# Projection stage of a transformer block in float32: its matmuls as three one-pass products of high and low parts, values made turned, keys and values kept in DRAM

## The reference, cut to what matters

```python
h = modulate(rms_norm(x, norm1_w), sh1, sc1)
hc = modulate(rms_norm(xc, norm1_w), csh1, csc1)
proj = h @ w_in                                   # q 512, k 128, v 128, hyena 1536 columns
kv_c = hc @ w_in[:, K_OFF:HY_OFF]                 # context keys and values
kc = rms_norm(split_heads(kv_c[..., :KV_W], N_KV_HEADS), k_norm_w)
q = rope_2d(rms_norm(split_heads(proj[..., :K_OFF], N_HEADS), q_norm_w), ang_r, ang_c)
k = rope_2d(rms_norm(split_heads(proj[..., K_OFF:V_OFF], N_KV_HEADS), k_norm_w), ang_r, ang_c)
v = split_heads(proj[..., V_OFF:HY_OFF], N_KV_HEADS)
att = windowed_attention(q, k, v, kc, vc, attn_sink)
hy = hyena_mixer(proj[..., HY_OFF:], ...)         # starts with a 3-tap convolution over the tokens
```

## Time and profile before

| | |
|---|---|
| median of 3 runs | 2721.09 us (2717.26 to 2721.49) |
| the profiled execution's own time | 2725.7 us |
| its span in the trace | 2723.9 us |
| mean granted clock of PE | 0.941 of full |
| busy: PE, PEld, DVE, ACT, POOL | 2376.9, 1452.7, 1333.2, 1097.9, 504.3 us |
| L800 (hyena products) | 768 matmuls, 336.0 us |
| L747 (key and query products) | 320 matmuls of 512 tokens, 142.7 us |
| L775 (values) | 288 matmuls, 28.9 and 3.7 us |

### The profile page before, as it was taken

How to read it: one execution, slowest core, us unless ns; L and a number is a source line. 1 busy time by engine, 2 the same in 40 slices (tenths; PEclk the granted TensorE clock), 3 DMA queues, 4 the chain that set the end, 5 groups by cost and what they waited for, 6 DMA issues and landing times. The chain is left out here.

```text
span 2723.9 us, 42063 instructions
## 1 busy us (share of the span) xinstructions
PE 2376.9 (87%) x14659; PEld 1452.7 (53%) x14660; DVE 1333.2 (49%) x2332; ACT 1097.9 (40%) x2039; POOL 504.3 (19%) x842
## 2 busy tenths in 40 slices
PE   4888999999996999858999999945988999889997
PEld 1333743444443666534666666643655666555664
DVE  4634376121121555434555555424655775555674
ACT  2543121111112444324554555414645665455563
POOL 1652011000000111000122222231222122222221
PEclk8988999999996999858999999967999999999999
DMA  4985121111117344241222222107988889786994
GB/s 162 333 258 144 30 78 43 39 54 47 31 47 184 87 111 110 51 150 54 58 64 60 66 69 71 51 31 284 319 271 285 290 301 324 237 262 210 313 317 125
DMA packets 239821, 410.02 MB, mean 151 GB/s; under 512 B 25220, under 2 KB 128140, under 8 KB 234884
## 3 DMA queue, kind: packets, MB, share of 16 engines
q1 hardware_dynamic: 161461, 334.11, 36.8%
q0 software_dynamic: 18608, 44.71, 6.9%
q10 hardware_dynamic: 59616, 29.38, 4.0%
HBM read 342.08 MB, written 74.49 MB: 153 GB/s over the span
## 5 line engine op out<-in xcount | busy, mean ns | idle before, releaser
L800 PE MATMUL ps_proj<-sb_hT,sb_win 128*128 128x512 f32 x768 | 336.0, 597 | 7.6 <-DVE sb_rot L906 6.0
L800 PEld LDWEIGHTS ps_proj<-sb_hT,sb_win 128*128 128x128 f32 x768 | 145.7, 192 | 189.8 <-issue 182.9
L2369 PE MATMUL ps_byp<-sb_w,sb_gT 128*128 128x512 f32 x512 | 232.8, 597 | 1.5 <-ACT sb_gT L2172 1.5
L2078 DVE TENSOR_TENSOR sb_w1l<-sb_raw,sb_w1h 128x1024 fp32r<-128x1024 f32 x128 | 148.2, 1220 | 172.8 <-ACT sb_w1h L2142 172.8
L1812 DVE CUSTOM_DVE_ANT_0 sb_pr<-ps_S,sb_mask 128x640 f32<-128x640 f32 x128 | 105.2, 822 | 128.5 <-PE ps_S L1636 128.5
L1634 PE MATMUL ps_S<-sb_kT,sb_qb 64*128 64x256 f32 x256 | 97.7, 465 | 67.1 <-DVE sb_mx L1812 49.6
L1731 ACT ACTIVATE sb_pr<-sb_pr,sb_nm 128x640 f32<-128x640 f32 x128 | 106.3, 830 | 117.8 <-DVE sb_nm L1816 117.8
L916 DVE TENSOR_SCALAR sb_hyv<-sb_hu,sb_cols 128x2048 f32<-128x2048 f32 x12 | 16.2, 1347 | 281.0 <-ACT sb_hu L869 281.0
L2078 DVE TENSOR_TENSOR sb_w3l<-sb_raw,sb_w3h 128x1024 fp32r<-128x1024 f32 x128 | 150.8, 1221 | 5.2 <-ACT sb_w3h L2142 5.2
L1346 POOL TENSOR_TENSOR sb_zr<-sb_zr,sb_skip 128x512 f32<-128x512 f32 x32 | 40.0, 1282 | 605.5 <-DMA sb_skip<-in_hy_skip 454.8
L747 PE MATMUL ps_proj<-sb_hT,sb_win 128*128 128x512 f32 x320 | 142.7, 600 | 8.9 <-DMA sb_win<-in_w_in 8.3
(11 more groups left out here) (292 smaller groups left out, 5007.7 us busy)
## 6 DMA issues: line engine op xcount, KB each, us to landing
sb_raw<-in_exp_w SPq DMA_DIRECT2D x64, 2048.0 KB, 17.0
sb_w<-in_exp_w SPq DMA_DIRECT2D x32, 2048.0 KB
sb_ada<-in_ada_w SPq DMA_DIRECT2D x16, 1536.0 KB, 7.8
scr_filt<-sb_fout ACTq DMA_DIRECT2D x128, 128.0 KB, 3.4
sb_yh<-scr_filt SPq DMA_DIRECT2D x64, 256.0 KB, 5.1
sb_win<-in_w_in SPq DMA_DIRECT2D x9, 1024.0 KB, 5.8
sb_xr<-in_x SPq DMA_DIRECT2D x16, 512.0 KB
sb_gt<-scr_hy_in SPq DMA_DIRECT2D x8, 1024.0 KB
```

What stands on the lines that cost most here:

```text
L800: ins = pe.matmul(mp[:, (NQ + n) % 4, :], w[:, pc % 3, k, (ct % 2) * P:(ct % 2 + 1) * P], g.hT[:, k, c * 512:(c + 1) * 512], start=(k == 0 ...
L2078: ve.tensor_tensor(piece(low[m], part), piece(raw13[par][:, m], part), piece(high[m], part).bitcast(F32), ALU.subtract).then_inc(lo[m], 1)
L2369: ins = pe.matmul(yp[:, part, :], gT[:, f, :], w2[par][:, f, part * 512:(part + 1) * 512], start=(f == 0), stop=(f == FT - 1), skip_group_ ...
```

## The change

All products of the stage are made of operands split in two parts: `high`, the value rounded to the one-pass type `float32r`, and `low`, the rest, also in that type. A product is then, for each of the 8 slices, `wh*high + wh*low + wl*high`: 24 instructions of one pass. What else changes:

- Splitting. ACT writes the high parts of the weights (`weights_high`) and of the rows (`rows_high`), DVE the low parts of the weights (`weights_low`) and of slices 0 to 4 of the rows, POOL those of slices 5 to 7 (`rows_low`). The low parts overwrite the originals. Modulation is now DVE's for slices 0 to 4 and POOL's for 5 to 7. The context comes first, then the chunks, and the later chunks are modulated and split between the rotations of the first key blocks (L942, L949 and L1020, L1027).
- The jobs are one list, which PE, ACT and DVE follow: context keys and values, then key and value chunks in alternation, then queries, then hyena. Values are made like all others and turned by PE (`turn_values`, L814).
- The root is taken by ACT from the mean square itself, straight from PSUM, with `eps` as its bias (`norm_root`), and the reciprocal comes after it on DVE; L895 is gone. In ACT's list `norm_root(m - 1)` stands behind `weigh(m)`, as before.
- Two weight pieces in place of three, one buffer for the convolution's input and one for its output in place of two, one for the turned result. `hcTh`, rope tables and the next stage's table `fwd` use the same memory one after the other, so the table is loaded only after the last rotation, and two more weight pieces wait behind it in SP's list.
- Keys and values go to DRAM, and `stage4` loads them back (four more transfers on SP, L1166) into memory that the rows had.

The core of the diff:

```diff
@@ stage3, order of the jobs
-    qk = [("k", 4, n) for n in range(CH)] + [("kc", 4, 0)] + [("q", ct, n) for ct in range(4) for n in range(CH)]
-    hy = [(ct, n) for ct in range(12) for n in range(CH)]
+    jobs = [("kc", 4, 0), ("vc", 5, 0), ("k", 4, 0), ("tc", 5, 0), ("v", 5, 0)]
+    for n in range(1, CH):
+        jobs += [("k", 4, n), ("t", 5, n - 1), ("v", 5, n)]
+    jobs += [("q", 0, 0), ("t", 5, CH - 1)] + [("q", ct, n) for ct in range(4) for n in range(CH)][1:]
+    jobs += [("h", 6 + ct, n) for ct in range(12) for n in range(CH)]
...
@@ PE, a product
-                for k in range(KT):
-                    rhs = g.hcT[:, k, :] if kind == "kc" else g.hT[:, k, c * 512:(c + 1) * 512]
-                    ins = pe.matmul(mp[:, n % 4, 0:N], w[:, pc % 3, k, (ct % 2) * P:(ct % 2 + 1) * P], rhs,
-                                    start=(k == 0), stop=(k == KT - 1))
+                if r == first_job[pc]:
+                    pe.wait_ge(w_lo, pc + 1)
+                if kind in ("kc", "k"):
+                    pe.wait_ge(lo_v, part + 1)
+                    pe.wait_ge(lo_p, part + 1)
...
+                for k in range(KT):
+                    a, b = wh[:, pc % 2, k, cs], wl[:, pc % 2, k, cs]
+                    pe.matmul(mp[:, r % 4, 0:N], a, high[:, k, :], start=(k == 0), stop=False)
+                    pe.matmul(mp[:, r % 4, 0:N], a, low[:, k, :], start=False, stop=False)
+                    ins = pe.matmul(mp[:, r % 4, 0:N], b, high[:, k, :], start=False, stop=(k == KT - 1))
...
@@ ACT
+            def weights_high(n):
+                act.wait_ge(ldw[n % 2], 16 * (n // 2 + 1))
+                act.copy(wh[:, n % 2, :, :], w[:, n % 2, :, :]).then_inc(w_hi, 1)
+            def rows_high(n):
+                x, high, _, _ = rows(n)
+                act.wait_ge(mod_v, n + 1)
+                act.copy(high[:, 0:5, :], x[:, 0:5, :]).then_inc(h_hi, 1)
+                act.wait_ge(mod_p, n + 1)
+                act.copy(high[:, 5:KT, :], x[:, 5:KT, :]).then_inc(h_hi, 1)
...
+            for job in jobs:
...
+                if kind in ("kc", "k", "q"):
+                    m = qk.index(job)
+                    weigh(m)
+                    if m >= 1:
+                        norm_root(m - 1)
...
+                if kind in ("vc", "v") and split <= CH:
+                    rows_high(split)
+                    split += 1
...
@@ DVE
+            modulate(0)
+            modulate(1)
+            rows_low(0)
+            weights_low(0)
+            modulate(2)
+            rows_low(1)
+            for n in range(NQ):
+                rotate(n)
+                if n + 3 <= CH:
+                    modulate(n + 3)
+                if n + 2 <= CH:
+                    rows_low(n + 2)
...
@@ POOL
+                    pool.dma_start(dst, src).then_inc(st_q[n % 2], 16)
+                if n + 3 <= CH:
+                    modulate(n + 3)
+                if n + 2 <= CH:
+                    rows_low(n + 2)
...
@@ stage4, SP, behind load_z(2)
+            for dst, src in ((g.kT[0:HD, :, P:P + T], g.k_dram), (g.kT[HD:2 * HD, :, 0:C], g.kc_dram),
+                             (g.v[:, 0:2, :], g.v_dram[:, NT:NT + 2, :]), (g.v[:, 3:3 + NT, :], g.v_dram[:, 0:NT, :])):
+                sp.dma_start(dst, src).then_inc(ld_kv, 16)
```

More of the change, by code:

```diff
@@ new lines, in stage3 @@
+    first_job = [min(at[job] for job in piece_of if piece_of[job] == n) for n in range(len(pieces))]
+    last_job = [max(at[job] for job in piece_of if piece_of[job] == n) for n in range(len(pieces))]
+    split_at = [None] + [min(first_job[n - 1] + 4, last_job[n - 1]) if n > 1 else at["k", 4, 2] for n in range(1, len(pieces))]
+    with e.stage() as st:
+        with nc.sbuf_tensor("sb_win", [P, 2, KT, PW], F32) as w:
+            pass
+        wl = e.sb(st, "winl", [P, 2, KT, PW], F32R)
+        wh = e.sb(st, "winh", [P, 2, KT, PW], F32R)
+        hh = e.sb(st, "hTh", [P, KT, T], F32R)
@@ new lines, in product @@
+            def product(job):
+                kind, ct, n = job
+                r, pc = at[job], piece_of[job]
+                part = n + 1 if kind in ("k", "v") else 0
+                cs = slice((ct % 2) * P, (ct % 2 + 1) * P)
+                if r == first_job[pc]:
[3 more added lines that the diff above has]
+                    pe.wait_ge(lo_p, part + 1)
+                bank(r)
+                if kind in ("kc", "vc"):
+                    high, low, N = hch, hcl, C
+                else:
+                    _, high, low, _ = rows(n + 1)
+                    N = 512
@@ new lines, in _ @@
+            normed = 0
+            for job in jobs:
+                kind, ct, n = job
+                if kind in ("tc", "t"):
+                    turn_values(job)
+                    continue
+                product(job)
+                if normed < NQ and at[qk[normed]] < at[job]:
+                    norm(normed)
+                    normed += 1
+                if kind == "h" and (ct, n) == (6, 0):
+                    pe.wait_ge(auxr, NQ)
+                    pe.wait_ge(root, NQ)
+                if kind == "h" and ct >= 7 and n == 1:
+                    turn(ct - 7)
@@ L872, in _ @@
             turned(11)
-            for b in range(2):
-                act.wait_ge(st_z[b], 16 * 6)
-            act.wait_ge(ld_f, 16)
+            act.wait_ge(st_z, 16 * 12)
         @block.vector
@@ L929, in _ @@
+            modulate(0)
+            modulate(1)
+            rows_low(0)
+            modulate(2)
+            rows_low(1)
             for n, (kind, ct, c) in enumerate(qk):
-                N = C if kind == "kc" else 512
+                N = width(kind)
                 pool.wait_ge(rotd, n + 1)
```

367 lines of the change are left out of this document (204 added, 163 removed).

## The result

| | before | after |
|---|---|---|
| median of the runs | 2719.18 us (4 runs, 2715.13 to 2721.49) | 2639.81 us (4 runs, 2628.94 to 2644.11) |
| ratio to before, 95% interval | | 0.9704 (0.9671 to 0.9736) |
| the profiled execution's own time, span | 2725.7, 2723.9 us | 2641.22, 2639.5 us |
| projection stage in its trace | 230.69 to 829.09: 598.4 us | 231.65 to 754.80: 523.1 us |
| first query product, from the stage's start | 81.1 us | 104.5 us |

The change is faster, by 79.4 us in the medians. The mechanism was the one forecast; sizes were off. The stage saves 75.2 us where 58.5 were forecast, and more than half of that difference lies in its start.

What follows compares the result with a forecast made beforehand. PE's matmul count and spacing were taken to bound the stage. Savings 20.6 + 5.2 + 65.2 less 32.5 made 58.5 us: 2725.7 to 2667.2, and 2662 as median, which lies 4.6 below the profiled execution; range 2640 to 2680.

Steps and rivals of the forecast that it cites:

- Costs 32.5: Stage start up to the first query product: 113.7 us after the change against 81.2 before, a loss of 32.5 us.
- the turns between DVE and POOL: Splitting a chunk at the start: DVE and POOL take turns at SBUF, holding both for 11.0 us a chunk.
- POOL's sending and products of the next rotation in between 1.5: Wait before key chunk 1: 1.5 us for this work, within 18.1 us from the end of key chunk 0.
- Key chunk 0: Key product at the stage's start: waits for 11.0 us of splitting from 14.3, starts 25.5, ends 31.1.
- Products behind gaps: Key products of chunks 1 to 3: PE's clock is low behind the gap, so 8.0 us for each product.
- 46 spacings, 0.2333 us each: Hyena and query products: expert stage's one-pass spacing carried over, 24 instructions in 5.60 us, saving 1.27 us a product.
- The queries: First query to first hyena product: 136.6 us before, 115.9 after, with DVE's work covered; saves 20.6 us.
- side by side: Rival, chance 0.28: DVE and POOL don't exclude each other or POOL modulates in 0.4; first query product at 99 to 101, 2648.
- Join: First to second hyena product: 14.8 us before, 9.6 after, as only the three rope products are waited for; saves 5.2 us.
- Next stage: Stage behind projection: four more transfers, 2.4 MB, priced 0 behind other loads, 8.4 us if the cover is gone.
- The cold laps: Rival, chance 0.08: DVE's waits inside query laps leave PE gaps, each lap loses up to 1 us: 2678.
- a larger spacing: Rival, chance 0.04: one-pass products in the stage spaced wider; the saving of 58.5 us is gone at 0.269 us.

Runs made afterwards that it cites:

- the second trace: The changed kernel run again with no edit, for a second trace: 2639.07 us, ratio 0.9719.

## Why the prediction was right and wrong

The stage saved 75.2 us where 58.5 were forecast. Of these 16.7 us 9.1 lie in the start, 5.5 in the hyena products, 2.2 in the queries, 0.3 behind the last product, and the join takes back 0.4. **The step that failed is the sum of the start, "Costs 32.5": 23.4 were measured.** The second one is the spacing of the products.

- **Start: mechanism right, 9.1 us too dear.** Low rows held PE up at each key product, as forecast, and in the key laps the turns between DVE and POOL were priced rightly (11.0 forecast, 10.7 measured in the lap of key chunk 0, 8.1 with DVE alone). Three terms were too large.
  - The gaps behind key chunks, 5.2 us in all. 3.0 of it is "POOL's sending and products of the next rotation in between 1.5", a term that stands in two laps and lies beside other work: POOL sent while DVE already modulated, and the next rotation's products stand behind the low rows in DVE's list, as the second excerpt of the order itself shows. From the end of key chunk 0 (260.5) reads, table load and root take until 263.7, reciprocal and product until 265.8, splitting until 276.6: 16.1 us, forecast 18.1; the next lap 16.8, forecast 19.0; the last two 12.2 and 8.3, forecast 12.8 and 8.7.
  - Key chunk 0 starts at 23.3 us, forecast 25.5. 0.4 of it is the first product; the rest is splitting, 9.4 us from the end of DVE's low weights (245.45) to that of the low rows (254.86), where full turns would make 2.3 + 2.26 + 3.40 + 2.8 = 10.8. Here DVE's and POOL's modulations alternated:

```profile
245.83 2.67 DVE L942 TENSOR_SCALAR sb_hT<-sb_hT,sb_scale,sb_mods 128x512 f32<-128x512 f32 x3
246.38 1.84 POOL L1020 TENSOR_SCALAR sb_hT<-sb_hT,sb_scale,sb_mods 128x512 f32<-128x512 f32 x2
```

  In the 1.84 us of POOL's two modulations DVE did two as well; one after the other the four would take 2 x (0.46 + 0.75) = 2.4. So POOL does not always keep DVE out between its instructions, and the turns overlap in part. What decides between this and the key laps, where DVE got in nowhere, is open.
  - Products behind gaps took 7.3, 7.2 and 7.7 us, forecast 8.0 each: 1.8 us. In the second trace they took 8.3, 7.7 and 8.0, so 8.0 was a fair price, and with it the start would still have been 7 us too dear.
- **Products: right in kind, mis-sized.** "46 spacings, 0.2333 us each" was carried from the expert stage; in the hyena products it is 0.2267, 5.44 us a product in place of 5.60. That is 7.5 over 47 products; 2 of them go to the lower clock behind the join (0.66 from 460 to 465 us), which the forecast left out, and which the second trace doesn't have: 70.7 measured against 65.2. The queries save 22.8 in place of 20.6: a lap is 7.21 us, not 7.32, the first two are shorter still (5.98, with a turn of values in place of a norm, and 6.87), and DVE's work stays under it. In the query laps the first matmuls behind the norm, from 349.61 to 351.47, still come 0.233 apart and later ones 0.2267. Waits between the matmuls don't make the difference, as the run that adds them shows.
- **The rival "side by side"** would have put the first query product at 99 to 101; the measured 104.5 is nearer to it than to 113.7, but for another reason. Its mechanism does not hold: in the key laps all of POOL's instructions hold DVE up for their full length, and POOL's modulation took 0.75 us, not 0.4. The Trainium skill (SBUF — State Buffer, Who interferes with whom) says that the second waits for the whole instruction, also where DVE has two SBUF inputs; this trace agrees: L972 took 3.31 us in place of 0.68, and the low part of the weights, 2048 columns, 3.90 us beside POOL and 2.28 alone:

```profile
241.55 3.90 DVE L953 TENSOR_TENSOR sb_winl<-sb_win,sb_winh 128x2048 fp32r<-128x2048 f32 x1
...
333.80 2.28 DVE L953 TENSOR_TENSOR sb_winl<-sb_win,sb_winh 128x2048 fp32r<-128x2048 f32 x1
```

  The alternating modulations at the start don't agree with it in full: whole turns would take 2.4 us there, and 1.84 were measured.

- **Join: right.** 4.8 us measured, 5.2 forecast; alone in the kernel before it gave 5.1.
- **Next stage: right.** Price 0 with cover, 8.2 measured without it, 8.4 forecast. The cold laps and a larger spacing did not come.
- **The sum.** With 75.2 in place of 58.5 the same working gives 2645.9. The 6 us left belong to no step: 1.9 are the median of before, which a fourth run moved from 2721.09 to 2719.18, and the other 4 are within the scatter of the stages behind, for which the range had no room. Since the result lies only 0.2 us below the range, this scatter decides on which side of its end it fell. Two slips of the working change little: 348.4 - 283.0 is 65.4, not 65.2, and the "1 to 5 us shorter" for a quicker modulation on POOL is 0.3 to 3.2, since the sum holds nine of them.

The forecast named the root that ACT takes late and priced the wait, but not what another order would give. ACT took the root of a block one product later than it could, and the low rows stood behind it. Undoing that is worth 19 us, as much as a quarter of what the change brings.

## What to carry to other kernels

When an instruction that feeds the bottleneck (here the low rows) stands in a list behind one that waits for something late (a rotation that waits for a root), follow that wait to the engine that holds it back; moving one instruction on ACT gave 19 us. Sharing elementwise work between DVE and POOL in SBUF gained nothing here, since in the key laps their times add up: eight modulations on DVE alone (3.73 us) were faster than five beside POOL (7.98). Before a difference of a few microseconds is put down to a change, compare two traces of the same kernel, in the stages that the change doesn't touch and inside the one that it does.

## What the runs showed of the hardware

- POOL instructions that follow one another can keep DVE waiting through all of them: 2.26 + 3.40 us showed up whole in DVE's 7.98, again in the next lap (8.07). It isn't always so: between 246.38 and 248.22 us the two engines alternated, two modulations each in 1.84 us, less than the 2.4 that they take one after the other.
- POOL's modulation of 512 float32 columns takes 0.75 us (2.26 for three), its subtraction of 1536 columns 3.40, DVE's of the same size 1.75.
- A DVE product with one input in PSUM (L971) took its usual 0.68 us beside POOL's subtraction; the next one, with both inputs in SBUF (L972), took 3.31.
- One-pass products of 512 columns follow each other at 0.2267 or at 0.2333 us, at a granted clock of 1.00 in both cases. Four waits and increments to a product leave 0.2267 as it is, and so does DMA traffic (0.2267 also between 470 and 475 us, at 306 GB/s). The cause of the difference is open.
- One and the same wait of 2.18 us at the join was followed by a fall of PE's granted clock (0.66 over 5 us) in one trace of the changed kernel and by none (1.00) in the other. Gaps cost more than their length: key products behind gaps of 8.5 and 9.0 us took 7.3 and 7.2 us, in the second trace 8.3 and 7.7, in place of 5.6.
